# Two norm weights folded into the output projection's weight rows, in a fused two-layer kernel

## What is computed

```python
    h = rmsnorm(x, pre_mix_norm[l])
    proj = h @ w_in[l]
    att = swa_sink_alibi(a_q, a_k, a_v, attn_sinks[l])
    ssd = ssd_mixer(s_z, s_xbc, s_dt, ..., ssd_norm_w[l])
    gdn = gdn_mixer(g_qkv, g_z, g_b, g_a, ..., gdn_norm_w[l])
    mix = jnp.concatenate([att, ssd, gdn], axis=-1) @ w_out[l]
    x = x + rmsnorm(mix, post_mix_norm[l])

# the end of ssd_mixer: g is [tokens, 2 groups, 256]
    g = g * lax.rsqrt(jnp.mean(g * g, axis=-1, keepdims=True) + EPS)
    return g.reshape(bsz, t, SSD_DIM) * norm_w

# the end of gdn_mixer: o is [tokens, 4 heads, 64]
    o = o * lax.rsqrt(jnp.mean(o * o, axis=-1, keepdims=True) + EPS) * norm_w
    o = o * jax.nn.silu(z)
```

## Time and profile before

| | before |
|---|---|
| median of 3 runs | 2251.5 us (2251.28 to 2252.94) |
| span of the profiled execution | 2258.5 us |
| TensorE busy | 2216.4 us, 98% |
| VectorE busy | 1581.9 us, 70% |
| ScalarE busy | 914.2 us, 40% |
| GpSimd busy | 263.5 us, 12% |
| granted TensorE clock, mean | 0.990 of full speed |

### The profile page before, as it was taken

One profiled execution on the slowest core, in us unless ns is written; L12 is line 12 of the kernel. 1 busy time (PEld: TensorE's weight loads), 2 busy tenths in 40 slices (PEclk: granted clock), 3 DMA queues, 4 the chain that ended last, 5 costly groups with the idle time before them and its releaser, 6 DMA issues. The chain is left out here.

```text
span 2258.5 us, 34288 instructions
## 1 busy us (share of the span) xinstructions
PE 2216.4 (98%) x13052; PEld 1823.0 (81%) x13052; DVE 1581.9 (70%) x2212; ACT 914.2 (40%) x1672; POOL 263.5 (12%) x266
## 2 busy tenths in 40 slices
PE   8999999999999999999999989999999999999997
PEld 7888888888888887887877777887888888888886
DVE  5657678876665545657687788887798777765557
ACT  5443544343343321243344445555533333324444
POOL 0222232100000000001232222322020000000000
PEclk9999999999999999999999989999999999999999
DMA  4111111144333264433233442323235444448655
GB/s 152 47 38 58 37 56 38 66 147 157 116 114 111 86 261 175 150 111 122 85 112 112 150 141 72 107 93 112 96 131 191 163 158 163 158 156 299 214 181 184
DMA packets 106952, 289.06 MB, mean 128 GB/s; under 512 B 9692, under 2 KB 35388, under 8 KB 102332
## 3 DMA queue, kind: packets, MB, share of 16 engines
q1 hardware_dynamic: 106812, 287.14, 36.2%
HBM read 205.01 MB, written 82.10 MB: 127 GB/s over the span
## 5 line engine op out<-in xcount | busy, mean ns | idle before, releaser
L124 PE MATMUL psG<-h_hi,w_hi 128*128 128x512 f32 (+1 forms) x624 | 164.4, 395 | 2.1 <-DVE features_T L1875 1.6
L124 PE MATMUL psG<-h_hi,w_lo 128*128 128x512 f32 (+1 forms) x624 | 161.6, 391 | 0.0
L124 PE MATMUL psG<-h_lo,w_hi 128*128 128x512 f32 (+1 forms) x624 | 161.4, 392 | 0.0
L455 POOL TENSOR_TENSOR sb_w<-sb_left 128x128 f32<-128x128 f32 (+3 forms) x96 | 96.9, 1014 | 320.3 <-DVE sb_left L582 320.3
L124 PEld LDWEIGHTS psG<-h_hi,w_hi 128*128 128x128 f32 x624 | 109.9, 188 | 23.7 <-DVE features_T L1875 2.9
L124 PEld LDWEIGHTS psG<-h_hi,w_lo 128*128 128x128 f32 x624 | 111.4, 188 | 20.2 <-DVE w_lo L155 0.2
L124 PEld LDWEIGHTS psG<-h_lo,w_hi 128*128 128x128 f32 x624 | 111.1, 188 | 20.1 <-issue 0.5
L582 DVE TENSOR_TENSOR_SCAN sb_left<-sb_left 128x128 f32<-128x128 f32 (+3 forms) x96 | 102.7, 1078 | 2.1 <-ACT sb_left L468 1.4
L150 ACT CAST w_hi<-w_raw 128x1024 fp32r<-128x1024 f32 x48 | 50.3, 1049 | 120.0 <-PE psG L124 61.7
L155 DVE TENSOR_TENSOR w_lo<-w_raw,w_hi 128x1024 fp32r<-128x1024 f32 x48 | 58.6, 1222 | 55.0 <-ACT w_hi L150 55.0
L2024 POOL TENSOR_TENSOR features_T<-m_bias_both 128x512 f32<-128x512 f32 x10 | 16.8, 1675 | 680.3 <-DMA m_bias_both<-in_proj_pairs 633.0
(11 more groups left out here) (657 smaller groups left out, 5949.8 us busy)
## 6 DMA issues: line engine op xcount, KB each, us to landing
w_raw<-in_units SPq DMA_DIRECT2D x76, 512.0 KB, 4.3
w_raw<-hidden_blocks SPq DMA_DIRECT2D x77, 256.0 KB, 2.9
merge_gates<-features_T SPq DMA_DIRECT2D x12, 1024.0 KB, 6.7
merge_gates<-merge_gates SPq DMA_DIRECT2D x12, 1024.0 KB, 4.8
features<-features_T SPq DMA_DIRECT2D x24, 512.0 KB, 3.8
w_spare<-in_units SPq DMA_DIRECT2D x22, 512.0 KB, 4.4
down_sums<-w_spare SPq DMA_DIRECT2D x22, 512.0 KB, 3.3
hidden_blocks<-features_T SPq DMA_DIRECT2D x11, 1024.0 KB, 3.9
```

Source lines behind the costliest of these rows:

```text
L124: return pe.matmul(out, lhs, rhs, start=first, stop=last, skip_group_check=True)
L455: pool.tensor_tensor(w, left_chunk(S, 1), left_chunk(S), ALU.subtract).then_inc(w_ready, 1)
```

## The change

The two norm weights become one vector of 1024 factors (ones for the 256 attention columns), laid out as 128x8 and loaded once. The splits of the six weight blocks that meet SSD and GDN columns multiply by it: ScalarE's copy gets a per-partition scale, VectorE's subtraction becomes a multiplication and a subtraction in one instruction. In the chain, ym0 and ym1 lose the norm row and become two scaled copies on ScalarE, directly behind yexp; TensorE's mtrm waits for them there. gzn goes: ogz reads the gate as ga wrote it. So that ga may be written while the gate of the tile before is still needed, gates lie in two buffers by turns, the first columns of GA in even stages and GZN in odd ones; in odd stages ga is two copies instead of one. The parameter row, loaded to all partitions in the phase before, shrinks from 612 to 36 columns.

```diff
-ROW = dict(bias=0, alog=12, sinks=24, dskip=28, ssd_norm=36, gdn_norm=548, end=612)
+ROW = dict(bias=0, alog=12, sinks=24, dskip=28, end=36)
...
+        GATE = [GA[:, 0:256], GZN[:]]
...
+            sp.dma_start(norm_w[:], out_norm).then_inc(norm_here, 16)
...
-                    scalF.wait(g, "ga", i)
-                    vectG.wait_last(g, "ogz", i)
-                    poolG.done("gzn", g.tensor_tensor(heads(GZN[:], GH), heads(GA[:, 0:256], GH), over(row("gdn_norm", 64), GH), ALU.mult))
...
-                    a.copy(w_hi[k][:], w_raw[k][:]).then_inc(w_hi_done, 1)
+                    if k < AH // 2:
+                        a.copy(w_hi[k][:], w_raw[k][:]).then_inc(w_hi_done, 1)
+                    else:
+                        a.wait_ge(norm_here, 16)
+                        a.activation(w_hi[k][:], w_raw[k][:], ACT.Copy, scale=norm_w[:, k:k + 1]).then_inc(w_hi_done, 1)
...
                     scalG.done("yexp", a.activation(yrr, yrr, ACT.Exp, scale=-0.5))
+                    scalG.wait(a, "yexp", i)
+                    for g in range(2):
+                        scalG.done(f"ym{g}", a.activation(M[:, 256 + 256 * g:512 + 256 * g], Y[:, 256 * g:256 * g + 256], ACT.Copy, scale=yrr[:, g:g + 1]))
...
-                    poolG.wait_last(a, "gzn", n)
+                    if n >= 2:
+                        vectG.wait(a, "ogz", n - 2)
                     poolF.wait_last(a, "vprev", n)
-                    scalF.done("ga", a.copy(GA[:], PS[:, 4, 0:384]))
+                    if n % 2 == 0:
+                        scalF.done("ga", a.copy(GA[:], PS[:, 4, 0:384]))
+                    else:
+                        a.copy(GATE[1], PS[:, 4, 0:256])
+                        scalF.done("ga", a.copy(GA[:, 256:384], PS[:, 4, 256:384]))
...
-                    tt(w_lo[k][:], w_raw[k][:], w_hi[k][:].bitcast(F32), ALU.subtract).then_inc(w_lo_done, 1)
+                    if k < AH // 2:
+                        tt(w_lo[k][:], w_raw[k][:], w_hi[k][:].bitcast(F32), ALU.subtract).then_inc(w_lo_done, 1)
+                    else:
+                        v.wait_ge(norm_here, 16)
+                        v.scalar_tensor_tensor(w_lo[k][:], w_raw[k][:], norm_w[:, k:k + 1], w_hi[k][:].bitcast(F32),
+                                               ALU.mult, ALU.subtract).then_inc(w_lo_done, 1)
...
-                if chain:
-
-                    scalG.wait(v, "yexp", i)
-                    tensG.wait_last(v, "mtrm", i)
-                    for g in range(2):
-                        c = slice(256 * g, 256 * g + 256)
-                        vectG.done(f"ym{g}", v.scalar_tensor_tensor(M[:, 256 + 256 * g:512 + 256 * g], Y[:, c], yrr[:, g:g + 1],
-                                                                    row("ssd_norm", 512)[:, c], ALU.mult, ALU.mult))
...
+                    if chain:
+                        scalG.wait(v, "ym1", i)
                     vectF.done("yo", tt(heads(Y[:], SH), heads(bank(4), SH), per(PT[:, PEA:PEA + SH], SH, 64), ALU.mult))
...
-                    poolG.wait(v, "gzn", i)
+                    scalF.wait(v, "ga", i)
                     tensH.wait_last(v, "mtrg", i)
-                    vectG.done("ogz", tt(M[:, 768:1024], OG[:], GZN[:], ALU.mult))
+                    vectG.done("ogz", tt(M[:, 768:1024], OG[:], GATE[i % 2], ALU.mult))
...
-                    vectG.wait(pe, "ym1", i)
+                    scalG.wait(pe, "ym1", i)
                     turn(tensG, "mtrm", 3, [M[:, c * P:(c + 1) * P] for c in range(6)])
...
+    norm_weights = np.concatenate([np.ones(256, np.float32), I["ssd_norm_w_2"][0], np.tile(I["gdn_norm_w_2"][0], GH)])
+    L["out2_norm"] = norm_weights.reshape(KC, P).T
```

More of the change, by code:

```diff
@@ L2178, in take, with layer2_mixers @@
         return t
-def layer2_mixers(nc, block, C, W, small, feats, acs_rows, D2, room_at, h_at, h_hi, h_lo, w_out, bias_in, x_in, g_post, g_pre, x_out, U0, PS, G):
+def layer2_mixers(nc, block, C, W, small, feats, acs_rows, D2, room_at, h_at, h_hi, h_lo, w_out, out_norm, bias_in, x_in, g_post, g_pre, x_out, U0, PS, G):
     with ExitStack() as ctx:
@@ L2220, in layer2_mixers @@
         sb = l[13].take
+        norm_w, norm_here = sb("out_norm", [P, KC]), sem("out_norm_here")
         PT, PSC, zero = sb("par", [P, PEND]), sb("state_decay", [P, 2]), sb("zero", [P, 1])
@@ L2261, in layer2_mixers @@
         scalF = Steps(sem("scalar_front"), "qk sq vb z ga lnr expr xs kt e0 e1 e2 e3 es pt")
-        scalG = Steps(sem("scalar_chain"), "T2 yq0 yq1 yln yexp T4 mtm T8 T16 T32 vu0 vu1 va vo1 vo0 T64 wt vn osq oln oexp")
+        scalG = Steps(sem("scalar_chain"), "T2 yq0 yq1 yln yexp ym0 ym1 T4 mtm T8 T16 T32 vu0 vu1 va vo1 vo0 T64 wt vn osq oln oexp")
         vectF = Steps(sem("vector_front"), "ss ssc nqk kb qg swab mx mx2 ngm sdif dsub dmask nc0 nc1 nc2 nc3 nt qkd sd0 sd1 den rden "
@@ L2266, in layer2_mixers @@
         vectX, vectN = Steps(sem("vector_xdt"), "xdt xdec"), Steps(sem("vector_blocks"), "m1 vt1 v0")
-        vectG = Steps(sem("vector_chain"), "V2 W2 ysc ym0 ym1 V4 W4 mlo V8 W8 V16 W16 vd0 vd1 vd2 vd3 VT64 oss osc og ogz")
+        vectG = Steps(sem("vector_chain"), "V2 W2 ysc V4 W4 mlo V8 W8 V16 W16 vd0 vd1 vd2 vd3 VT64 oss osc og ogz")
         vectD, vectH = Steps(sem("vector_state"), "s0 s1 s2 s3"), Steps(sem("vector_turned"), "mglo")
         poolF = Steps(sem("gpsimd_front"), "par keep0 keep1 xd kprev nm vbt vprev")
-        poolG = Steps(sem("gpsimd_chain"), "kbg kd pes gzn qgt qkdc")
+        poolG = Steps(sem("gpsimd_chain"), "kbg kd pes qgt qkdc")
         tensP, tensA = Steps(sem("tensor_product"), "p0 p1"), Steps(sem("tensor_a6"), "a6")
@@ L4258, in layouts @@
     rows = [I["ssd_dt_bias_2"][0], I["gdn_dt_bias_2"][0], I["ssd_A_log_2"][0], I["gdn_A_log_2"][0], I["attn_sinks_2"][0],
-            I["ssd_D_2"][0], I["ssd_norm_w_2"][0], I["gdn_norm_w_2"][0]]
+            I["ssd_D_2"][0]]
+    norm_weights = np.concatenate([np.ones(256, np.float32), I["ssd_norm_w_2"][0], np.tile(I["gdn_norm_w_2"][0], GH)])
+    L["out2_norm"] = norm_weights.reshape(KC, P).T
     L["rows"] = np.concatenate(rows).reshape(1, -1)
@@ L4317, in build @@
                 with nc.Block() as block:
-                    mixed = layer2_mixers(nc, block, C, W, small, feats, acs_rows, D2, feat_at, h_end - 8 * KC * T, *h, A["w_out2"], A["attn_bias"],
+                    mixed = layer2_mixers(nc, block, C, W, small, feats, acs_rows, D2, feat_at, h_end - 8 * KC * T, *h, A["w_out2"], A["out2_norm"], A["attn_bias"],
                                           x1, A["post_mix_norm_2"], A["pre_ffn_norm_2"], x2, UNIT0["ffn"], PS, G)
```

## The result

The changed kernel took 2260.4 us (median of 11 runs, 2257.4 to 2262.3), the kernel before beside it 2253.7 (11 runs, 2251.3 to 2260.5). The ratio is 1.0025, with a 95% interval of 1.0015 to 1.0035: slower by 5.6 us, or 3.4 to 7.9. Forecast were 2255.8 us and 4.3 us more than before; the forecast time is 4.6 us too low, inside the range. Of all executions, those of the experiments included, three (3128, 6630 and 11968 us) are left out of every number.

The account below looks back on a forecast made before the run. TensorE was taken to set the pace in settled stages, with the T4 copy's margin deciding. Settled stages 1.84, stage 1 0.55, stage 2 0.8 and last stage 1.15 made 4.3 us; 2251.5 + 4.3 = 2255.8 us, range 2248.5 to 2262.

Parts of the forecast that it names:

- What bounds the kernel: Settled stages of the layer-2 mixers: TensorE, busy 35.00 of 35 us, sets the pace; relief of VectorE or GpSimd gives nothing.
- the rival that rests on VectorE's relief: Stages 1 and 2 gain if ScalarE hides both ym: 2249.4 us, 2242.8 without the clock's fall; chance 0.10.
- it does nothing that counts: Rival: ym fits into ScalarE's idle time and the T4 copy is in time, 2251.5 us; chance 0.06.
- ym on ScalarE: Between yexp and z on ScalarE: two ym make z, ga and T4 0.95 us later, bounds 0.7 and 1.05.
- ga in two buffers: Odd stages: one copy of 384 columns becomes 256 and 128, about 0.08 us longer, between 0 and 0.2.
- GpSimd's product gone: Without gzn, ysc is freed and yln starts 0.19 us earlier in stages 4 to 7; xd and nqk end later.
- Settled stages: Stages 3 to 7: TensorE waits at X4 0.32 us in 4 and 6, 0.40 in 3, 5, 7; sum 1.84.
- The margin of 0.44: Settled stages: the T4 copy on ScalarE can come 0.44 us later before TensorE's X4 weights wait for it.
- Stages 1, 2 and the last: Losses of 0.55 us (0.2 to 0.9), 0.8 (0.3 to 0.9) and 1.15 (0.6 to 1.3) in these stages.
- Weights and DMA: Weight splits on ScalarE and VectorE, and the smaller parameter load: 0 taken, at most 0.3 us each.
- The step that missed: Base of the forecast: runs' median 2251.5 us, with the profiled span's 7.0 us excess carried as a difference.
- The rival of a further fall of the clock: A second fall to 1.2 GHz, in stage 2, costs 6.6 us: 2262.4 us; chance 0.14.

Follow-up runs that it names:

- the repeated one: The kernel before, unchanged, profiled once more beside the experiments: ratio 1.0000 (0.9989 to 1.0011); its profiled execution took 2256.2 us.

## Why the prediction was right or wrong

**What bounds the kernel** was right: TensorE in settled stages. Taking VectorE's work away gave idle time (0.94 to 2.22 us before V4), and the rival that rests on VectorE's relief fell with it; "it does nothing that counts" fell with X4's wait. The rule of the Trainium skill, VectorE: DVE Perf Modes, section "Rules for kernel authors", to minimise the count of chained operations would have given 2243.8. The 16 instructions fewer on VectorE gave nothing here, where VectorE was off the path.

**ym on ScalarE.** Taken at 0.95 for both; measured 0.93 in even stages (odd ones, with ga's part, 0.98). An ym takes 0.50 us:

```profile
L2548 ACT ACTIVATE m_mix<-m_y,small_cols x16: 492/502/512, 1316.9 to 1568.2; 128x256 f32<-128x256 f32 x16
```

That line of the changed kernel bears out the row of the nearest form. The Trainium skill, ScalarE: Activation LUTs, section "Rules for kernel authors", which speaks of up to about three times per element in bf16, would by my estimate have made it 1.44; in float32 here ScalarE's 0.50 stands against VectorE's 0.48 with the row and 0.35 without.

**ga in two buffers.** 0.08 for odd stages was taken, 0.05 measured.

**GpSimd's product gone.** ysc is free of its hold in stages 3 to 7, as forecast. In stage 2 it is the other way round: there ysc takes 0.67. nqk is held by the later xd in stages 1 to 7, 1.35 each, as forecast. The prediction's reading of the rows, that the two engines exclude each other when both read two SBUF tensors, is too narrow: ysc, which is held, reads one (small_cols).

**Settled stages.** X4's wait over the gap is 0.30 in stages 4 and 6 and 0.36 in 3, 5 and 7, for 0.32 and 0.40. The sum 1.93 for 1.84 hides that stage 7 alone lost 0.7, half of it not at X4 (0.25 of that lies in the cut: the ysc of the last stage comes later against TensorE); the other four lost 0.26 to 0.34. So 1.84 was met in part by luck. The margin of 0.44 is the number that carried the forecast, and three kernels put it to the test from different sides: half of the delay costs nothing, a delay without the move costs what exceeds 0.44, and the stages shorten by just the start-to-start time of a product put ahead of X4.

**Stages 1, 2 and the last.** 0.7, 0.6 and 1.3 for 0.55, 0.8 and 1.15. V4 in stage 1 is 0.44 late against ysc (0.47 forecast). The 0.30 of yx that was set against it is not to be had in that stage: the yx of 0.99 starts at 1310.3, before stage 1. In stage 2 the margin of 0.63 belonged to the execution of the rows; in the repeated one X4's weights start 0.33 behind the copy, with no margin. V4 there is 0.10 late and the end of nqk 0.49, for 0.32 and 0.8, so 0.6 for 0.8 bears out nqk's part and not X4's. In the last stage the delay is 0.94 and the margin 0.15, as taken; the hold by the moved GpSimd copies is 0.23 instead of 0.35, as yq0's wait shows (0.57 before), and what they hold is ogz (L2966):

```profile
L2966 DVE TENSOR_TENSOR m_mix<-m_sqo,m_ga x4: 630/632/634, 1345.5 to 1563.7; 128x256 f32<-128x256 f32 x4
...
1565.81 0.42 ACT L2541 ACTIVATE m_mix<-m_y 128x256 f32<-128x256 f32 x1 [0.80 <-DVE m_y L2972]
```

An ogz took 0.42 in the kernel before. 0.94 + 0.23 - 0.15 = 1.02 is the growth of X4's wait, of the forecast 1.15.

**Weights and DMA** cost nothing: the kernel with ym on VectorE has them and loses nothing.

**The step that missed** is the base: "The profiled span is 2258.5 us, 7.0 above the runs' median of 2251.5; I carry the difference". The three runs were at the fast end of before, whose median over 98 executions is 2254.8, and the profiled execution was at its slow end, with 20.5 us at 1.2 GHz. The 0.52 of that stretch was in the rows, and I used it for a rival but not to ask whether other executions had it. Of the 4.6 us that the forecast time was too low, 3.3 are the base by all executions (2.2 by those beside the changed kernel, 2253.7), and 1.4 go with the lower clocks of the changed kernel's runs. The sum of the terms was right within the noise: 4.3 forecast, 4.1 at equal clock, 4.7 between the two traces.

**The rival of a further fall of the clock** gave 2262.4, near the measured time, but its mechanism was not seen: the changed kernel's one stretch in stages 1 and 2 has the same place and length as that of the repeated before. The forecast's own times ended at 2257.8; that 2260.4 lies in the range is owed to this rival's end of it, and so is luck. One of the prediction's signs of being wrong came true as it was put, that the stretch at 1.2 GHz changes length: 23.9 us in the execution of the rows, 13.8 now. The repeated before shows that before does so by itself. Whether the change makes the fall likelier is open. The mean clock was 0.9927 for the changed kernel, 0.9938 for before and 0.9954 with ym on VectorE, but also 0.9928 with one ym on each engine, which has no wait at X4 in settled stages.

No version beat the kernel before beyond its interval. The two that come nearest keep the root scaling on VectorE, without the row: 0.9991 with the SSD row alone folded and 0.9992 with both; at equal clock neither differs from before (+0.1 and -0.5).

## What to carry to other kernels

Before work moves to an idle engine, look for the instruction behind it in that engine's queue for which the bounding engine waits next, and measure its margin in two rows; only what exceeds the margin is paid, and the relief of an engine that waits is nothing. Place the moved work behind that instruction if its reader allows. Ask what a base of three runs and one profile stands for: where the profile shows a stretch at the lower clock, the runs may have it or not, and that can be more than the change.

## What the runs showed of the hardware

The granted clock of one and the same program differs between executions, from 0.990 to 0.997 on average, and with it the time by 9 us (0.4%); TensorE is busy 98% of the time. In two executions the long stretch at 1.2 GHz lay in stage 1 (20.5 us) and in stage 2 (13.7 us). The Trainium skill, TensorE: Matmul & The Clock Gate, section "What's actually happening", says that the gate's window is free-running and not started by the kernel, so that the point where the clock changes varies between runs. The spread agrees with that; no run here shows the gate's phase.

Without its second tensor operand VectorE's 128x256 product in float32 fell from 0.48 to 0.35 us. The Trainium skill, VectorE: DVE Perf Modes, section "The perf-mode tier table", puts `tensor_scalar`, the form without the row, at 2x in float32 and `tensor_tensor` at 1x; the form with the row, SCALAR_TENSOR_TENSOR, is not in it. The trace agrees in direction, with 0.73 of the time and not half.

VectorE's nqk (0.69 us when nothing disturbs it, 1.35 beside xd) ends 0.55 behind xd's end where xd goes first, as in stage 4 of the changed kernel and in the kernel with z and ga in pieces. Where the two start within 0.02 us (odd stages with ym behind T4), nqk goes first in 0.65, and xd takes 1.58 instead of 1.04. A 128x512 product on TensorE, 0.40 long in its record, follows the one ahead after 0.22 to 0.23 at the full clock. And a ScalarE copy of 128 columns took 0.43 instead of 0.28 behind copies of 64 columns.
